# A two-block fp32 model kernel: the sparse-attention stage in another order, and filler matmuls ahead of the norm transposes

## The reference, cut to what matters

```python
def nsa_mixer(h, cos, sin, w_in, q_norm, k_norm, cmp_pe, cmp_w1, cmp_b1, cmp_w2, cmp_b2, w_out):
    q, kc, vc, ks, vs, kw, vw, gates = jnp.split(h @ w_in, splits, axis=-1)   # 1024, 6 x 256, 48
    q = rmsnorm(q.reshape(B, S, H, dh), q_norm)                               # 16 heads of 64
    q_rot = apply_rope(q, cos, sin)
    ks = apply_rope(rmsnorm(ks.reshape(B, S, Hk, dh), k_norm[1]), cos, sin)   # 4 key heads
    kw = apply_rope(rmsnorm(kw.reshape(B, S, Hk, dh), k_norm[2]), cos, sin)
    ...
    def compress(t, i):          # 15 blocks of 32 tokens, 16 apart; each flattened to 2048
        ...
        blocks = blocks + cmp_pe[i][:, None, :]
        hid = jax.nn.gelu(blocks @ cmp_w1[i] + cmp_b1[i])                     # 2048 x 256
        return hid @ cmp_w2[i] + cmp_b2[i]
    kc = rmsnorm(compress(kc, 0), k_norm[0])
    vc = compress(vc, 1)
    # scores of q (not rotated) with the 15 compressed keys, softmax, o_c
    # q_rot with ks (blocks chosen by score), q_rot with kw: softmax, o_s, o_w
    o = gates[..., 0:1] * o_c + gates[..., 1:2] * o_s + gates[..., 2:3] * o_w
    return o.reshape(B, S, H * dh) @ w_out
```

## Time and profile before

| what | value |
|---|---|
| time, median of 3 (lowest to highest) | 3508.07 us (3506.81 to 3508.25) |
| the profiled execution: its own time | 3508.96 us |
| its span, first to last instruction | 3507.0 us |
| mean granted TensorE clock | 0.959 of full |
| busy: TensorE, VectorE, ScalarE, Pool | 94%, 55%, 45%, 4% |
| sparse stage: first projection matmul to first head | 2464.1 to 2618.8, 154.7 us |
| heads, then w_out | to 2673.9, to 2701.5 |

### The profile page before, as it was taken

One profiled execution on the slowest core, in us unless ns is written; L12 is line 12 of the kernel. 1 busy time (PEld: TensorE's weight loads), 2 busy tenths in 40 slices (PEclk: granted clock), 3 DMA queues, 4 the chain that ended last, 5 costly groups with the idle time before them and its releaser, 6 DMA issues.

```text
span 3507.0 us, 48865 instructions
## 1 busy us (share of the span) xinstructions
PE 3282.8 (94%) x19206; PEld 2817.0 (80%) x19206; DVE 1928.8 (55%) x2159; ACT 1562.3 (45%) x1825; POOL 136.5 (4%) x151
## 2 busy tenths in 40 slices
PE   8987799899899999989999999999769999998899
PEld 6886787788778888978888888888657888898787
DVE  4456655655554546655455554555665555484554
ACT  4447344444544445434444444444335444463443
POOL 0000000100000003120000000000000000003000
PEclk9998899899999999899999999999979999998999
DMA  6542355355255555405555545565411655652164
GB/s 210 191 121 82 95 191 179 126 182 190 79 186 188 172 183 171 128 14 168 189 182 180 178 155 187 171 196 191 150 49 49 193 178 192 187 159 78 53 194 138
DMA packets 423766, 535.41 MB, mean 153 GB/s; under 512 B 21122, under 2 KB 370798, under 8 KB 423632
## 3 DMA queue, kind: packets, MB, share of 16 engines
q1 hardware_dynamic: 421840, 528.76, 47.3%
q0 software_dynamic: 1792, 4.72, 0.6%
HBM read 532.36 MB, written 1.05 MB: 152 GB/s over the span
## 4 chain that ended last, share of the span: by engine, by line
PE 90%; DVE 6%; ACT 3%; issue 1%; DMA 0%; SPq 0%; ACTq 0%; DVEq 0%
PE banks L133 23%; PE banks L135 23%; PE banks L134 23%; PE banks L130 3%; PE banks L131 3%; PE banks L132 3%; PE banks L312 2%; PE banks L1666 2%; PE banks L247 1%; DVE w_lo L114 1%; ACT w_hi L106 1%; PE banks L1616 1%; PE banks L1123 1%; PE banks L1111 1%; ACT xT_hi L191 0%
## 5 line engine op out<-in xcount | busy, mean ns | idle before, releaser
L114 DVE TENSOR_TENSOR w_lo<-raw,w_hi 128x2048 fp32r<-128x2048 f32 x514 | 1176.3, 2294 | 664.6 <-ACT w_hi L106 664.6
L106 ACT ACTIVATE w_hi<-raw 128x2048 fp32r<-128x2048 f32 x514 | 982.0, 1915 | 599.6 <-PE banks L135 494.0
L133 PE MATMUL banks<-w_hi,xT_hi 128*128 128x512 f32 (+3 forms) x2736 | 1054.7, 385 | 76.9 <-issue 33.2
L135 PE MATMUL banks<-w_hi,xT_lo 128*128 128x512 f32 (+3 forms) x2736 | 1040.1, 380 | 0.0
L134 PE MATMUL banks<-w_lo,xT_hi 128*128 128x512 f32 (+3 forms) x2736 | 1039.0, 380 | 0.0
L133 PEld LDWEIGHTS banks<-w_hi,xT_hi 128*128 128x128 f32 x2736 | 524.7, 192 | 173.7 <-issue 39.0
L135 PEld LDWEIGHTS banks<-w_hi,xT_lo 128*128 128x128 f32 x2736 | 523.8, 191 | 96.5
L134 PEld LDWEIGHTS banks<-w_lo,xT_hi 128*128 128x128 f32 x2736 | 524.9, 192 | 90.8
L133 PE MATMUL banks<-w_hi,hidT_hi 128*128 128x512 f32 x1056 | 411.9, 390 | 0.0
L135 PE MATMUL banks<-w_hi,hidT_lo 128*128 128x512 f32 x1056 | 411.1, 389 | 0.0
L134 PE MATMUL banks<-w_lo,hidT_hi 128*128 128x512 f32 x1056 | 410.9, 389 | 0.0
(11 more groups left out here) (407 smaller groups left out, 2411.0 us busy)
## 6 DMA issues: line engine op xcount, KB each, us to landing
raw<-ffn_w_gate_up SPq DMA_DIRECT2D x352, 512.0 KB
raw<-ffn_w_down SPq DMA_DIRECT2D x264, 512.0 KB
raw<-ffn_w_gate SPq DMA_DIRECT2D x88, 512.0 KB
raw<-ffn_w_up SPq DMA_DIRECT2D x88, 512.0 KB
raw<-gdn_w_in SPq DMA_DIRECT2D x64, 512.0 KB
raw<-sc_w_in SPq DMA_DIRECT2D x24, 512.0 KB
...
```

The costliest lines, as they stand in the source:

```text
L106: c.nc.scalar.activation(c.w_hi[r][:], c.raw[r][:], ACT.Copy).then_inc(c.sem("w_hi_split"), 1)
L114: c.nc.vector.tensor_tensor(c.w_lo[r][:], c.raw[r][:], c.w_hi[r][:].bitcast(F32), ALU.subtract).then_inc(c.sem("w_lo_split"), 1)
L133: mm(out, x_hi, w_hi, start=start, stop=False)
L135: return mm(out, x_lo, w_hi, start=False, stop=stop)
```

## The change: what it does

It has two parts. The first: `pe_norm` sends 14 or 28 bf16 matmuls of 128 x 384 (28 where the source stage has a norm of its own) ahead of the transposes of the norm; their result is not read. It does so in front of every stage but the first and those feed-forward stages that follow a stage without `post`: 28 in front of six stages (recurrence, ffn2, shared keys and values, ffn1, forgetting attention, ffn2) and of the first stage of the second block, and 14 in front of its four mixers.

The second: the sparse stage is put into another order. The projection of kc and vc comes first, then that of q (two steps), w1k and w1v, that of ks, vs, kw and vw (two steps), the gates. The blocks are not gathered: TensorE brings the tokens of an even and an odd head into the two halves of the partitions by a transpose and a plain fp32 product with the identity, shifted by a column, and the compressing projections read them with a stride (65 rows, the last of which holds the position term, so that it becomes a bias). The squares of q and of the keys are taken by ScalarE from PSUM, the scaled values by VectorE from PSUM (`normed`), the gains go into the tables of the rotation (`turn`), the rotations run on Pool (`rotate`), the values are copied by ScalarE, keys reach both halves of the partitions by the same pair of operations as the tokens, and the transposes and products of the compressed softmax stand inside the heads (`beside_heads`). Slab splits are called one at a time between these parts (`next_split`).

```diff
+BUSY_MATMULS = 14
...
 def pe_norm(c, pe, st):
...
     src = c.h if st.kind == "ffn" else c.xn
+    if n and (st.kind != "ffn" or st.source.post is not None):
+        for _ in range(BUSY_MATMULS if st.source.post is None else 2 * BUSY_MATMULS):
+            c.nc.tensor.matmul(c.bank[NORM_BANKS[1]][:, 0:3 * P], c.ident_bf[:], c.causal_bf[:], start=True, stop=True)
     for m, t in PARTS:
...
+    def rotate(x, dst, heads, j, t):
+        by_cos, by_sin = v.turn[j]
+        a, b = (v.tmp[i][:, 0:heads * HEAD_DIM].rearrange("p (h a d) -> p h a d", a=2, d=32) for i in range(2))
+        x = x.rearrange("p (h a d) -> p h a d", a=2, d=32)
+        step(g.tensor_tensor(out=a, in0=x, in1=by_cos[:, t].unsqueeze(1).broadcast_to([P, heads, 2, 32]), op=ALU.mult), False)
+        step(g.tensor_tensor(out=b, in0=x[:, :, ::-1, :], in1=by_sin[:, t].unsqueeze(1).broadcast_to([P, heads, 2, 32]),
+                             op=ALU.mult))
+        step(g.tensor_tensor(out=dst.rearrange("p (h a d) -> p h a d", a=2, d=32), in0=a, in1=b, op=ALU.add))
+    pool.wait_ge(c.sem("projection_read"), w_q.step + 1)
...
+    for s in range(2):
+        pool.wait_ge(c.sem("projection_read"), w_q.step + s + 1)
+        for t in range(TOKS):
+            at = slice(512 * s, 512 * (s + 1))
+            rotate(v.p[:, t, at], v.qr[:, t, at], HEADS // 2, 0, t)
+        assert n[0] == NSA_ROPED[s]
+    for s, lo in enumerate((KS, KW)):
...
+        for t in range(TOKS):
+            x = v.p[:, t, lo:lo + N_KV * HEAD_DIM]
+            rotate(x, x, N_KV, 1 + s, t)
...
+    def compressed_tokens():
...
+        pe.wait_ge(c.sem("projection_read"), w_c.step + 1)
+        for n, bank in enumerate(blk_banks):
+            lo = (KC, VC)[n // 2] + n % 2 * 2 * HEAD_DIM
+            for j in range(2):
+                for t in range(TOKS):
+                    src = v.p[:, t, lo + j * HEAD_DIM:lo + (j + 1) * HEAD_DIM]
+                    at = j * SEQ + t * P
+                    even, odd = row_halves()
+                    tr(c.bank[bank][even, at:at + P], src, c.ident[:])
+                    skip = 0 if at else 1
+                    last = mm(c.bank[bank][odd, at + skip - 1:at + P - 1], src, c.ident[:, skip:P], start=True, stop=True)
+            last.then_inc(c.sem("nsa_c_transposed"), 1)
+    def block_rows(i):
+        def operand(k):
+            at = slice(k, BLK - CMP_STRIDE + k + 1, CMP_STRIDE // 2)
+            return v.blk_hi[:, i, at], v.blk_lo[:, i, at]
+        return operand
...
+    def keys(lo, group, bank):
+        for h in (2 * group, 2 * group + 1):
             for t in range(TOKS):
...
+                src, at = v.p[:, t, lo + h * HEAD_DIM:lo + (h + 1) * HEAD_DIM], h % 2 * SEQ + t * P
+                even, odd = row_halves()
+                tr(c.bank[bank][even, at:at + P], src, c.ident[:])
+                last = mm(c.bank[bank][odd, at:at + P], src, c.ident[:], start=True, stop=True)
+        last.then_inc(c.sem("nsa_transposed"), 1)
+    def beside_w_q(s):
+        if s == 0:
+            compressed_tokens()
...
+    def beside_w_kv(s):
+        if s == 0:
+            pe.wait_ge(c.sem("projection_read"), w1v.step + 1)
...
+            last.then_inc(c.sem("nsa_hid_transposed"), 1)
+            queries(v.p, 0, b1)
+            queries(v.p, 1, b1 + 4)
+            return
+        pe.wait_ge(c.sem("nsa_hidden"), 1)
...
+        last.then_inc(c.sem("nsa_compressed"), 1)
+        pe.wait_ge(c.sem("projection_read"), w_kv.step + 1)
+        queries(v.p, 2, b2)
+        queries(v.p, 3, b2 + 4)
+        pe.wait_ge(c.sem("nsa_brought"), 1)
+    pe_project(c, pe, w_c, norm=st.norm)
+    pe_project(c, pe, w_q, after=beside_w_q)
+    pe.wait_ge(c.sem("nsa_blk_lo"), 5)
+    pe_project(c, pe, w1k, operand=block_rows(0))
+    pe_project(c, pe, w1v, operand=block_rows(1))
+    pe_project(c, pe, w_kv, after=beside_w_kv)
+    pe_project(c, pe, w_gates)
+    pe.wait_ge(c.sem("nsa_pool"), NSA_ROPED[1])
+    pe.wait_ge(c.sem("nsa_brought"), 3)
+    queries(v.qr, 0, b1 + 4)
+    queries(v.qr, 1, b2)
...
     last.then_inc(c.sem("nsa_kc_transposed"), 1)
+    pe.wait_ge(c.sem("projection_read"), w_kv.step + 2)
+    queries(v.qr, 2, b0)
+    queries(v.qr, 3, b0 + 4)
...
+    pe.wait_ge(c.sem("nsa_pool"), NSA_ROPED[2])
+    pe.wait_ge(c.sem("nsa_brought"), 6)
+    keys(KS, 0, b1 + 4)
+    keys(KS, 1, b2)
+    pe.wait_ge(c.sem("nsa_pool"), NSA_ROPED[3])
+    pe.wait_ge(c.sem("nsa_brought"), 7)
+    keys(KW, 0, b2 + 4)
+    keys(KW, 1, b0)
+    pe.wait_ge(c.sem("nsa_brought"), 12)
...
+    def beside_heads(part):
+        if part == 0:
+            pe.wait_ge(c.sem("nsa_c_probs"), 1)
+            for t in range(TOKS):
+                for g in range(N_KV):
+                    last = tr(c.bank[6 + t][:, g * P:(g + 1) * P], v.p[:, t, KC + g * P:KC + (g + 1) * P], c.ident[:])
+                last.then_inc(c.sem("nsa_transposed"), 1)
+            pe.wait_ge(c.sem("nsa_brought"), 14)
+            combined(0)
+            return
+        pe.wait_ge(c.sem("nsa_c_added"), 1)
+        combined(1)
+        pe.wait_ge(c.sem("nsa_c_added"), 2)
+    pe_heads(c, pe, nsa_heads(c), st.heads, beside_heads)
...
+    def squares(pr, s, n):
+        act.wait_ge(c.sem("slab_used"), pr.slab + 2 * s + 2)
+        bank = (pr.step + s) % 3
+        for t in range(TOKS):
+            last = scalar.activation(v.sq[:, t, 0:n], c.bank[bank + 4 * t][:, 0:n], ACT.Square)
+        last.then_inc(c.sem("nsa_squares"), 1)
...
+    def root(j):
+        act.wait_ge(c.sem("nsa_ms"), j + 1)
+        part = v.kc_ms[0:N_CMP] if j == 4 else v.ms[:, :, ms_cols(j)]
+        scalar.activation(part, part, ACT.Sqrt).then_inc(c.sem("nsa_root"), 1)
...
+    def mean_squares(j, n):
+        dve.wait_ge(c.sem("nsa_squares"), j + 1)
+        part = v.ms[:, :, ms_cols(j)]
+        for t in range(TOKS):
+            last = vector.tensor_reduce(part[:, t], v.sq[:, t, 0:n].rearrange("p (h d) -> p h d", d=HEAD_DIM), AX, ALU.add)
+        chain(last)
+        tsc(part, part, 1.0 / HEAD_DIM, EPS, ALU.mult, ALU.add).then_inc(c.sem("nsa_ms"), 1)
+    def normed(pr, s, j, at, n):
+        dve.wait_ge(c.sem("nsa_root"), j + 1)
+        part, bank = v.ms[:, :, ms_cols(j)], (pr.step + s) % 3
+        chain(vector.reciprocal(part, part))
+        if pr is w_kv:
+            dve.wait_ge(c.sem("nsa_values"), TOKS * (s + 1))
+        for t in range(TOKS):
+            last = tt(v.p[:, t, at:at + n].rearrange("p (h d) -> p h d", d=HEAD_DIM),
+                      c.bank[bank + 4 * t][:, 0:n].rearrange("p (h d) -> p h d", d=HEAD_DIM), over(part[:, t], HEAD_DIM),
+                      ALU.mult)
+        last.then_inc(c.sem("projection_read"), 1)
+    dve_split(c, dve, next_split(w_q, 0, 0))
...
+    for n, bank in enumerate((b0, b0 + 4, 3, 7)):
+        dve.wait_ge(c.sem("nsa_blk_hi"), n + 2)
+        at = slice(n % 2 * SEQ, (n % 2 + 1) * SEQ)
+        tt(v.blk_lo[:, n // 2, at], c.bank[bank][:, 0:511:2], v.blk_hi[:, n // 2, at].bitcast(F32), ALU.subtract
+           ).then_inc(c.sem("nsa_blk_lo"), 1)
+    dve_split(c, dve, next_split(w_q, 1, 0))
+    mean_squares(1, 512)
+    normed(w_q, 1, 1, 512, 512)
+    dve_split(c, dve, next_split(w_q, 1, 1))
     dve_project(c, dve, w1k, lambda s, view: copy(v.hid_rows[0], view))
...
+    def combined():
+        for t in range(TOKS):
+            dve.wait_ge(c.sem("nsa_c_out"), t + 1)
+            for b in range(2):
+                last = copy(v.p[:, t, b * 512:(b + 1) * 512], c.bank[2 + b][:])
+            last.then_inc(c.sem("nsa_c_added"), 1)
+        dve.wait_ge(c.sem("nsa_c_added"), 2)
+        dve_split(c, dve, next_split(w_kv, 1, 1))
+    dve_heads(c, dve, nsa_heads(c), st.heads, combined)
+    dve_split(c, dve, next_split(w_gates, 0, 0))
...
-    sparse = Stage("nsa", projections=[wide(w_nsa, 0, 5), P_(w_nsa, GATES, 1, "tok", width=3 * HEADS),
-                                       P_(w_cmp[0], 0, 1, "rows", slabs=2, operand_cols=(0, CMP_COLS)),
-                                       P_(w_cmp[1], 0, 1, "rows", slabs=2, operand_cols=(CMP_COLS, 2 * CMP_COLS)),
+    sparse = Stage("nsa", projections=[wide(w_nsa, KC, 1), wide(w_nsa, 0, 2),
+                                       P_(w_cmp[0], 0, 1, "rows", slabs=2, operand_cols=(0, CMP_ROWS)),
+                                       P_(w_cmp[1], 0, 1, "rows", slabs=2, operand_cols=(0, CMP_ROWS)),
+                                       wide(w_nsa, KS, 2), P_(w_nsa, GATES, 1, "tok", width=3 * HEADS),
                                        wide(w["nsa_w_out_2"][0], 0, 2)])
```

More of the change, by code:

```diff
@@ L1214, in dve_heads @@
     maxima(1)
+    if beside is not None:
+        beside()
     for i in range(pairs):
@@ L2289, in dve_nsa @@
-    last.then_inc(c.sem("nsa_c_dup"), 1)
     dve.wait_ge(c.sem("nsa_small_loaded"), 128)
```

409 lines of the change are left out of this document (195 added, 214 removed).

## The result

The changed kernel takes 3484.56 us (median of 4 runs, 3482.51 to 3485.24) against 3508.16 us, a ratio of 0.9935 (95% interval 0.9922 to 0.9947). That is 23.6 us faster, where 44 were forecast, and outside the range of 3452 to 3480.

What follows compares the result with a forecast made beforehand. TensorE was taken as the bound, with its idle and half-clock time mostly in the sparse stage. From 3508.96 us, 41 gained there and 3.3 at the edges gave 3464.7, against the median 3464 us; range 3452 to 3480.

Steps and rivals of the forecast that it cites:

- The bound: TensorE is 90% of the chain; time is won only where it idles or runs at half clock, mainly the sparse stage.
- the new wait: Sparse stage, between the slabs of w1k and w1v: TensorE waits 6.7 us for splits, bounds 4 and 9.
- the price of Pool's instructions: Rotations on Pool: 1.27 us for each 128 x 512 instruction, 0.7 for half that size, 24.5 us with a memset.
- VectorE and Pool hold each other: Splits beside the rotations: each engine waits for the other's running instruction, about 1 us and 0.8 in the stall.
- the cover over norms and rotations: Sparse stage: norms, rotations and copies cost nothing under ks, kw and gates, 27 us of TensorE; q's rotations have 40.
- the loss at the edge into ffn1: Fillers before ffn1, where TensorE waits only 0.7 us, start the projection later: 3.9 us lost, bounds 3.2 and 5.6.
- the fillers: Matmuls ahead of the norm transposes warm the clock at the stage edges: 3.3 us won in sum, bounds -7 and +5.
- Rival (d): Sparse stage rotations on Pool so slow that the kernel is slower than before; 3 in 100.
- a pair is 0.33 to 0.5; I take 0.33: Tokens and keys: one transpose plus one plain fp32 product in us; 16 pairs 5.2 for tokens, 5.3 for keys.
- the full speed that I counted for everything behind the gates: Sparse stage at full clock: rotated q and compressed keys 2.2 us, scores 3.4, keys 5.3.
- rival (b): Sparse stage's small work at half clock, 10 to 14 us more, or Pool at twice its price; about 3477 us, 10 in 100.
- the part moved into the heads: Transposes, products and copies of the compressed softmax inside the heads: 6.3 us.

Runs made afterwards that it cites:

- e3: Changed kernel with the transposes and identity products of tokens and keys taken in groups of four instead of in turn: 3471.97 us, ratio 0.9898.
- e11: Changed kernel with the transposes of the token and key pairs turned into plain identity products, still in turn between the halves: 3470.51 us, ratio 0.9892.
- e14: Grouped kernel (e3) with the transposes turned into plain identity products, four of the lower half, then four of the upper: 3472.21 us, ratio 0.9904.
- e8: Changed kernel with keys and tokens doubled by VectorE and transposed, w1v split first, waits slab by slab, no fillers before ffn1: 3455.19 us, ratio 0.9853.
- e5: Changed kernel without the 28 fillers at the edge into ffn1 behind the shared keys and values: 3480.74 us, ratio 0.9921.
- e2: Changed kernel without the fillers, only the sparse stage in the new order: 3486.79 us, ratio 0.9937.
- e4: Changed kernel with groups of 8 bf16 matmuls added at five places inside the sparse stage to keep the clock up: 3485.29 us, ratio 0.9934.

## Why the prediction was wrong

**What was right.** The bound (TensorE, with its idle time in the sparse stage), the place and length of the new wait (6.7, measured 5.5), the price of Pool's instructions (1.27 to 1.3 us, 0.73 for the half size, for which I took 0.7) and that VectorE and Pool hold each other, the cover over norms and rotations (no wait of TensorE on Pool), and the loss at the edge into ffn1 (3.9, measured 4.4). Of the fillers I forecast 3.3 us; the medians give 2.2 (with the order) and 2.7 (alone), neither clear of the noise. Rival (d) was nowhere near.

**Two steps failed,** both terms of the stage's sum. The first is "a pair is 0.33 to 0.5; I take 0.33". I added a transpose's spacing in a row of transposes to a product's spacing in a row of products. In turn they take 0.59, outside my bounds too: 32 pairs are 8.4 us more at the full clock. e3 (0.39, by groups) and e11 (0.23, products alone) show that it is the change from the one to the other, and e11 with e14 that it isn't the column halves.

**The second,** and by its size the larger, is the full speed that I counted for everything behind the gates, and with it the weight of rival (b). The clock is 0.50 for 34.1 us (2556.4 to 2590.5): rotated q, compressed keys and scores take 11.3 us in place of 2.2 + 3.4, the keys 6.2 us over their 9.5 at full clock, and the part moved into the heads, 2588.9 to 2598.2, 9.3 us with the first pair's transposes in place of 6.3. That is 12 us to the first head and, by the first two pairs' scores (4.7 us, 2.6 in e11 at the full clock), some 3 behind it: a little over the 10 to 14 that (b) had. I had argued against (b) from one stretch in which 2.8 us of transposes were followed by a full clock, and gave 10 in 100 to what came.

By the Trainium skill's rule that transposes do not count as busy (TensorE: Matmul & The Clock Gate, Part 4) this rival was to be expected. The runs do not show that the rule is the reason. In the changed kernel the clock fell in the gates' products, 5 us behind the last transpose; in e11 there is not one transpose in the keys or scores, and the clock was still 0.50 for 20.5 us, which began in the gates and took in 64 products of 15 columns; in e8 sixteen transposes follow four slabs at 1.00. Nor is the stretch fixed by the code. The sparse stage of e5 is the changed kernel's, and in its execution the clock came back for the scores and fell again in front of the keys:

```profile
2557.20:2560.70 3.50, 3.50 (x19) 2.90 (x17) 0.36 (x2) 1.79 (x3) 1.94 (x3) 0.51 0.01 2
2560.70:2564.10 3.40, 3.40 (x61) 3.35 (x60) 0.00 (x0) 2.16 (x3) 0.00 (x0) 0.99 0.00 0
2564.10:2584.50 20.40, 19.71 (x71) 8.87 (x71) 5.25 (x15) 6.07 (x7) 0.00 (x0) 0.50 0.00 1
```

So why the clock falls there stays open; that it did, and what it cost, is shown.

**The sum again.** To the first head 103.4 forecast, 122.3 measured: tokens +4.3, keys +10.4, q and scores +5.7, stall -1.2, the last copy -0.3. The other terms came to 79.7 where 79.6 stood, and that is partly luck: w1k took 6.2 in place of 5.3 and w1v 7.3 in place of 6.8, and the wide slabs with the gates some 1.3 less than before. In the heads' beginning some 4 more, and the 2 that I took off for hand-overs were not needed. That is the 41 less 21 = 20 us which the stage gave; e2 has 21.8 for it.

**Range and chances.** The range held the pair at 0.5 and the clock as two cases, never both. By these numbers the pair alone would have given some 3472 us and the clock alone some 3479; together they leave the range. They are two terms: e4 has the dear pair at the full clock, e11 the cheap pair with 20.5 us at the half.
